# Differential attention in a two-layer block: scores from split queries and keys in three fp32r passes

## The reference, cut to what matters

```python
def diff_attention(h, w_qkv, lam, subln_g, w_o, t5_table, lambda_init):
    q, k, v = jnp.split(h @ w_qkv, 3, axis=-1)
    # 8 heads, each with 2 maps of 64 dimensions; 512 positions
    ...
    def block_fn(args):                      # 128 queries at a time
        ...
        s = jnp.einsum('bhmqd,bhmkd->bhmqk', qb, k).astype(jnp.float32) + bias[None, :, None]
        a = jax.nn.softmax(s, axis=-1)
        w = a[:, :, 0] - lam_full * a[:, :, 1]
        return jnp.einsum('bhqk,bhkd->bhqd', w.astype(v.dtype), v)
```

## Time and profile before

| | |
|---|---|
| median of 3 runs | 2231.64 us (2231.15 to 2233.04) |
| profiled execution, its own time | 2231.41 us |
| its span | 2229.6 us |
| PE busy | 2165.4 us, 97% of the span |
| DVE busy | 1280.8 us, 57% |
| ACT busy | 896.0 us, 40% |
| scores of differential attention (L1209) | 36.8 us in 128 records |

### The profile page before, as it was taken

One profiled execution on the slowest core, in us unless ns is written; L12 is line 12 of the kernel. 1 busy time (PEld: TensorE's weight loads), 2 busy tenths in 40 slices (PEclk: granted clock), 3 DMA queues, 4 the chain that ended last, 5 costly groups with the idle time before them and its releaser, 6 DMA issues. The chain is left out here.

```text
span 2229.6 us, 35501 instructions
## 1 busy us (share of the span) xinstructions
PE 2165.4 (97%) x14014; PEld 1719.0 (77%) x14014; DVE 1280.8 (57%) x1653; ACT 896.0 (40%) x1405; POOL 119.8 (5%) x96
## 2 busy tenths in 40 slices
PE   8999999999999999999999999999898899999999
PEld 6787788888876677778888887777787566888887
DVE  6564576663377777566665347686456476333333
ACT  4444532222364566642222244655222444323221
POOL 0000011110000000001111000000233000000000
PEclk9999999999999999999999999999999999999999
DMA  7331233333323222123233331322000111333321
GB/s 254 104 112 59 76 114 95 100 97 95 95 78 111 82 72 67 52 72 113 94 94 104 95 94 57 102 76 85 3 4 4 47 39 58 113 94 97 101 94 66
DMA packets 52933, 187.65 MB, mean 84 GB/s; under 512 B 5840, under 2 KB 6096, under 8 KB 52688
## 3 DMA queue, kind: packets, MB, share of 16 engines
q1 hardware_dynamic: 52528, 185.39, 26.6%
q10 hardware_dynamic: 288, 0.59, 0.1%
HBM read 183.86 MB, written 2.10 MB: 83 GB/s over the span
## 5 line engine op out<-in xcount | busy, mean ns | idle before, releaser
L297 PE MATMUL l_banks<-l_r_hi,l_w_hi 128*128 128x512 f32 x1440 | 573.9, 399 | 2.9 <-DVE l_r_lo L1748 2.3
L299 PE MATMUL l_banks<-l_r_hi,l_w_lo 128*128 128x512 f32 x1440 | 561.2, 390 | 0.0
L298 PE MATMUL l_banks<-l_r_lo,l_w_hi 128*128 128x512 f32 x1440 | 561.1, 390 | 0.0
L282 DVE TENSOR_TENSOR l_w_lo<-ring,l_w_hi 128x1024 fp32r<-128x1024 f32 x216 | 299.0, 1386 | 106.7 <-ACT l_w_hi L276 102.9
L276 ACT ACTIVATE l_w_hi<-ring 128x1024 fp32r<-128x1024 f32 x216 | 227.0, 1055 | 290.6 <-PE l_banks L299 285.9
L297 PEld LDWEIGHTS l_banks<-l_r_hi,l_w_hi 128*128 128x128 f32 x1440 | 270.6, 188 | 72.6 <-issue 8.9
L298 PEld LDWEIGHTS l_banks<-l_r_lo,l_w_hi 128*128 128x128 f32 x1440 | 270.8, 188 | 57.0 <-issue 3.6
L299 PEld LDWEIGHTS l_banks<-l_r_hi,l_w_lo 128*128 128x128 f32 x1440 | 270.5, 188 | 57.3
L297 PE MATMUL ff_banks<-ff_r_hi,ff_w_hi 128*128 128x512 f32 x512 | 200.0, 391 | 0.0
L299 PE MATMUL ff_banks<-ff_r_hi,ff_w_lo 128*128 128x512 f32 x512 | 199.2, 389 | 0.0
L298 PE MATMUL ff_banks<-ff_r_lo,ff_w_hi 128*128 128x512 f32 x512 | 199.2, 389 | 0.0
(11 more groups left out here) (505 smaller groups left out, 3221.5 us busy)
## 6 DMA issues: line engine op xcount, KB each, us to landing
ring<-weights SPq DMA_DIRECT2D x315, 512.0 KB, 3.6
na_bias<-window_bias SPq DMA_DIRECT2D x16, 512.0 KB, 5.4
da_rel<-t_rel SPq DMA_DIRECT2D x8, 448.0 KB, 4.3
X<-xT SPq DMA_DIRECT2D x8, 256.0 KB, 5.6
outT<-X SPq DMA_DIRECT2D x8, 256.0 KB, 2.1
const<-consts SPq DMA_DIRECT2D x1, 1312.0 KB, 11.2
l_pt<-pT SPq DMA_DIRECT2D x2, 512.0 KB, 4.7
kr<-mla_consts SPq DMA_DIRECT2D x1, 512.5 KB, 6.0
```

Source lines behind the costliest of these rows:

```text
L282: dve.tensor_tensor(self.w_lo[:, c % self.slots, :], k.ring[:, g % RING, :], self.w_hi[:, c % self.slots, :].bitcast(F32), ALU.subtract).t ...
L297: pe.matmul(psum, hi, self.hi(rhs_slot), start=start, stop=False)
L298: pe.matmul(psum, hi, self.lo(rhs_slot), start=False, stop=False)
L299: return pe.matmul(psum, lo, self.hi(rhs_slot), start=False, stop=stop)
```

## The change

The queries and keys of each head are split into a rounded part and a rest. ACT writes the rounded part (`round_qk`) to a new tensor `qk_hi` of four 128x512 tiles, which lies in the memory of the first four tiles of `X`. DVE writes the rest (`split_qk`) over `qb` and `kb` themselves. `score(n)` becomes three passes of two float32r matmuls: high by high, high query by low key, low query by high key. Since `X[0:4]` is overwritten, SP stores these tiles to the output tensor in HBM at the start of the stage and loads them back after the last score; the tail waits for them before it adds. The first score of a head waits for both splits of the head.

```diff
+        with ExitStack() as under:
+            self.qk_hi = under.enter_context(nc.sbuf_tensor("qk_hi", [P, 4, S], F32R))
         self.X = self.sb("X", [P, DT, S])
...
             if c == FIRST:
                 buffers_free(sp)
+                for j in range(4):
+                    sp.dma_start(k.dram["outT"][j * P:j * P + P, :], k.X[:, j, :]).then_inc(x_kept, 16)
                 sp.dma_start(lam[:, :, :], ...).then_inc(lam_loaded, 16)
...
+        sp.wait_ge(x_kept, 64)
+        sp.wait_ge(scored, NBLK)
+        for j in range(4):
+            sp.dma_start(k.X[:, j, :], k.dram["outT"][j * P:j * P + P, :]).then_inc(k.x_loaded[j], 16)
...
             if i == 0:
-                pe.wait_ge(evacuated, AT[1, h] + 1)
+                pe.wait_ge(qk_split, 2 * h + 2)
             if n:
                 pe.wait_ge(added, n)
-            for m in range(2):
-                mm = pe.matmul(s_ps[:, m, :], qb[half(m), h % 2, i * P:i * P + P], kb[half(m), h % 2, :], start=True, stop=True)
+            qh, kh = hi[:, 0:2, :], hi[:, 2:4, :]
+            ql, kl = lo
+            for part, (q, key) in enumerate(((qh, kh), (qh, kl), (ql, kh))):
+                for m in range(2):
+                    mm = pe.matmul(s_ps[:, m, :], q[half(m), h % 2, i * P:i * P + P], key[half(m), h % 2, :], start=part == 0, stop=part == 2)
             mm.then_inc(scored, 1)
...
+        def split_qk(c):
+            kind, h = ORDER[c]
+            if kind < 2:
+                dve.wait_ge(qk_rounded, ROUNDED.index(c) + 1)
+                dve.tensor_tensor(lo[kind][:, h % 2, :], (qb, kb)[kind][:, h % 2, :], hi[:, 2 * kind + h % 2, :].bitcast(F32), ALU.subtract).then_inc(qk_split, 1)
...
             elif n < NBLK:
                 for c in chunks_of(n):
                     evacuate(c)
+                for c in chunks_of(n):
+                    split_qk(c)
             if n < NBLK:
                 add_bias(n)
...
+        def round_qk(c):
+            kind, h = ORDER[c]
+            if kind < 2:
+                act.wait_ge(evacuated, c + 1)
+                if c == 0:
+                    act.wait_ge(x_kept, 64)
+                act.activation(hi[:, 2 * kind + h % 2, :], (qb, kb)[kind][:, h % 2, :], ACT.Copy).then_inc(qk_rounded, 1)
...
                 for c in chunks_of(n):
                     round_ahead(c)
+                    round_qk(c)
...
+                    if norm == 0 and j < 4 and x_back:
+                        dve.wait_ge(k.x_loaded[j], x_back)
                     dve.tensor_tensor(k.X[:, j, :], k.X[:, j, :], m[:, j, :], ALU.add).then_inc(s["added"], 1)
```

More of the change, by code:

```diff
@@ L1107, in differential @@
     LAG_T, LAG_O = 2, 6
+    hi = k.qk_hi
+    with ExitStack() as under:
+        lo = [under.enter_context(k.nc.sbuf_tensor(f"da_{n}", [P, 2, S], F32R)) for n in ("ql", "kl")]
     qb, kb, vb = (sb(n, [P, 2, S]) for n in ("qb", "kb", "vb"))
@@ L1125, in differential @@
     (x_squared, gathered, x_summed, lned, rstd_done, evacuated, lam_loaded, prep, lam_exped, scored, added, maxed, exped, inverted,
-     halved, mixed, turned, t_free, weighed, o_out, squared, summed, ms_out, rs_done, normed, out_rounded, out_split) = (st.sem(f"da_{n}") for n in (
+     halved, mixed, turned, t_free, weighed, o_out, squared, summed, ms_out, rs_done, normed, out_rounded, out_split, x_kept, qk_rounded, qk_split) = (st.sem(f"da_{n}") for n in (
          "x_squared", "gathered", "x_summed", "lned", "rstd_done", "evacuated", "lam_loaded", "prep", "lam_exped", "scored", "added",
          "maxed", "exped", "inverted", "halved", "mixed", "turned", "t_free", "weighed", "o_out", "squared", "summed", "ms_out",
-         "rs_done", "normed", "out_rounded", "out_split"))
+         "rs_done", "normed", "out_rounded", "out_split", "x_kept", "qk_rounded", "qk_split"))
     rel_loaded = [st.sem(f"da_rel_loaded{n}") for n in range(2)]
@@ L1299, in evacuate @@
             split(c + SLOTS)
+        ROUNDED = [c for c in range(N) if ORDER[c][0] < 2]
+        def split_qk(c):
[3 more added lines that the diff above has]
+                dve.tensor_tensor(lo[kind][:, h % 2, :], (qb, kb)[kind][:, h % 2, :], hi[:, 2 * kind + h % 2, :].bitcast(F32), ALU.subtract).then_inc(qk_split, 1)
         def add_bias(n):
@@ L1343, in vector @@
                     evacuate(c)
+                for c in chunks_of(0):
+                    split_qk(c)
                 dve.wait_ge(lam_exped, 1)
@@ L1482, in layer_tail @@
     gate_bank = [1, 2, 3, 5, 6, 7, 4, 5]
+    x_back = (0, 32)[layer]
     gains = [(f"g{layer}1", f"g{layer}2"), (f"g{layer}3", f"g{layer}4")]
```

## The result

The changed kernel takes 2245.03 us (median of 4 runs, 2243.67 to 2245.43) against 2232.11 us before (4 runs, 2231.15 to 2233.04): 1.0062 of the time before, 95% interval 1.0050 to 1.0074, so 12.9 us slower. The profiled execution has a span of 2241.9 us, 12.3 more than before.

What follows compares the result with a forecast made beforehand. PE was taken to bound the stage, DVE close behind and binding at some blocks. Score gains less DVE's splits gave +1.5 to +1.6 us by block 19, three stalled heads +5.1: +6.6, so 2238.5 us, range 2235 to 2253.

Steps and rivals of the forecast that it cites:

- three stalls of 2.4 us: First scores at blocks 20, 24, 28: PE waits for K's split, queued behind DVE's weight split; 7.3 us together.
- matmuls one behind another: Rival for the score on PE: float32r halves run in series, 0.41 us lost per score, 2252 us; chance 0.15.
- the side by side case: Score on PE: float32r halves overlap, a pair takes 0.228 us; gains of 0.1 to 0.4, clock kept, chance 0.52.
- The score itself: 32 scores on PE: each 0.90 us in place of 1.15, a gain of 0.25, 8.0 us in all.
- the sign: Starts of the score's six matmuls on PE: pairs within 0.01 us, 0.23 us from pair to pair.
- The rule of the Trainium skill: Rival for the score: weight loads of the same row group show, gain 0 per score, 2242.5 us; chance 0.05.
- The mix: PE's transposes waiting for DVE's mix in the stage: total wait grows from 3.9 us to some 8.
- the walk: Block-by-block account of PE and DVE lateness: 1.9 us by block 7, +1.5 to +1.6 by 19, +6.6 at last score.
- X out and back: Stores of four X tiles at the stage's start and loads after the last score: covered by other work, cost nothing.
- the rounding on ACT: 16 roundings of Q and K on ACT, 9.6 us, hidden under DVE's weight split of 1.23 us.
- The rival: Clock falls in the stalls at blocks 20, 24, 28: three falls cost 5.1 us, 2243.5 us; chance 0.14.
- the prediction's own sign: Condition for being wrong: PE's clock shows below 1.00 between 705 and 905 us.

## Why the prediction was right, and where it was off

The direction was right, and the time lies within the range: 2245.03 us in 2235 to 2253. The likeliest value was 2238.5, 6.9 us over the kernel before, of a loss of 12.9: about half. The cause named first, three stalls of 2.4 us by the order on DVE, is shown. That the time fell inside the range is in part luck: the upper end stands for matmuls one behind another, which did not come. That end was also added up too low: with the 0.30 us at the ends that the side by side case has, six passes take 1.67 us and not 1.56, and the serial case would be some 2256. Point by point:

- **The score itself.** The halves run side by side, as taken. The gain is 0.17 per score and not 0.25: I had set the ends at 0.98 and 0.68 us for the place and chosen 0.90, and the measured place is 0.98. The losses at the ends stayed what they were in float32. That is the mis-sized term, 32 x 0.08 = 2.6 us on PE. The pairs do not all follow at 0.23 us, as the sign had it: the second comes 0.34 us after the first. The rule of the Trainium skill (TensorE: Matmul & The Clock Gate, Part 3), by which weight loads of the same rows would not be hidden, is not borne out: the third pair follows the second at 0.23 us, on the same rows.
- **The three stalls.** Forecast 2.4 us each at blocks 20, 24 and 28; the rows show 2.38, from the very order named. Taking K earlier removed them, and 3.4 us came back at the same blocks as waits for the mix, while as much went elsewhere; the total fell by 7.1 us. At block 0 the wait is 0.4 us, as forecast.
- **The mix.** Forecast 3.9 rising to some 8 us; measured 7.7. The passes alone bring it to 5.7 and the splits with float32 scores to 5.8, so the splits make about half of the rise and the faster scores the other half.
- **What the walk left out.** It let the transposes wait for the mix alone. They also wait for ACT's evacuation of V's transposes and of the weights', 1.4 us before and 3.8 after, 2.4 us more. These rows were in the waits of the kernel before, at 0.6 and 0.8 us, and I did not follow them. They are another way in which DVE's lateness reaches PE, through ACT's wait for the inversion. Here the walk left its path: at block 10, where it had DVE catch up, PE waits 1.0 us for V's transposes, and at block 14 the changed kernel is 2.2 us behind and not 0.4.
- **X out and back**, and the rounding on ACT, were costed at nothing. The first is shown by its own run; of the second, the run with the rounding on POOL shows 1.7 us less wait at most.
- **The clock.** The rival had it fall in the three stalls. It fell behind one, block 28, and there slowed the score and the transposes; in return the fall of before at the last score did not come. Inside the stage the balance is near zero. By the prediction's own sign, a clock below 1.00 between 705 and 905 us, the clock kept through the stage was wrong. The 2.5 us behind the stage, in code that the change doesn't touch, go in part with the longer stretches near 1400 and 1760 us (1.7 us at most, since one stretch of before is missing). The forecast had ended with "behind it DVE and PE take the same steps as before", which is right for the steps and wrong for their time. Why the clock falls there twice as long after a shift of some 10 us is not shown by any run; that the number and places of the stretches differ with every edit is, and that the mean clock differs between runs of one program.

Together, for the profiled span: 6.6 us were forecast and 12.3 measured. Up to block 19 the changed kernel loses 1.8 us more than the walk has, by the waits not followed and the smaller gain. From there to the last score it loses 2.5 more: 1.0 by the smaller gain of 12 scores, 1.5 by the clock at block 28. Behind the last score it gains 1.5, as the fall of before is missing; 2.5 lie behind the stage and 0.3 ahead of it. The passes alone kept 1.8 of their 5.4 us, so PE's gain is worth about a third here.

## What to carry to other kernels

Where an engine's gain comes with work for its neighbours, look for the instruction whose consumer stands closest behind it, and put the new work beyond that place; here three stalls of 2.4 us came from 16 small operations in one order and went with one number in the schedule. A split of 0.61 us more on DVE costs nothing or all of itself, by which wait ends last there, so walk every wait in the list of waits and not only the longest. And judge an edit by its stage's waits as well as by the total, and look at the mean clock of the profiled execution beside that of the other runs: changes of the clock were worth as much as the smaller effects, in one profile more than in the rest.

## What the runs showed of the hardware

- Two float32r matmuls that contract 64 partitions each, on the two halves of the partitions, start within 0.01 us of each other and run as a pair in the time of one of 128: 0.23 us for 512 columns from the second pair to the third, whose weight loads run under the second.
- Going in and out of such a group costs 0.30 us: the place of three pairs is 0.98 us, with 0.09 us ahead of the first pair, 0.11 between the first and the second, and 0.09 behind the third.
- POOL working beside DVE lengthens DVE's 128x1024 subtraction from 1.23 to 1.57 us on average, and up to 2.2 us where POOL's own subtraction of 128x512 (1.4 us) runs beside it. POOL's rounding alone hardly does: 1.24 us on average, with one of the 24 at 1.48.
- The stretches at half clock, 3.4 us or 6.8 us, repeat to 0.1 us in two profiled executions of one program at the same mean clock (0.995) and come at other places when the program is edited far ahead of them. Over all runs of the changed kernel the mean clock is 0.991 to 0.995, and the time goes with it: 2249.8 us at the lowest, 2240.6 at the highest.
